# The order of the small matmuls of two half-height heads in the attention stages: pairs side by side, or one head after the other

## The chip, the cores and the metric

The kernel runs on one core of a Trainium2 chip. The metric is device time of one launch, in microseconds (us), the median of the runs. A lower time is better.

## The reference

A decoder of three layers on one sequence of 256 tokens with 1024 features, all in fp32. Layer one: a conformer convolution, cross attention to a memory of 256 tokens, a gated MLP. Layer two: differential attention, cross attention, a gated MLP. Layer three: a sparse attention of 16 heads, then a gated MLP with a short convolution. Two of the attentions matter here, and both have heads of 64 features:

```python
# differential attention: 8 heads, each with two score maps, causal
s = einsum('bqhcd,bkhcd->bhcqk', q, k) * 64 ** -0.5          # c = 0, 1
p = softmax(where(k_pos <= q_pos, s, -inf))
a = p[:, :, 0] - lam * p[:, :, 1]
o = einsum('bhqk,bkhe->bqhe', a, v)                          # e = 128 wide

# third layer: 8 heads with three branches (compressed keys, selected blocks,
# window 512), gated and added, and 8 heads with a window of 128 and a sink
o_nsa = g0 * o_cmp + g1 * o_slc + g2 * o_win
o_swa = banded_attention(qw, kw, v_sw, 128, sinks)
```

With 256 tokens the selected blocks are all blocks and the window of 512 holds all tokens, so that "selected" and "window" are both plain causal attention, each with keys and values of its own. The compressed branch has 15 keys.

## The kernel before

Activations lie transposed in SBUF, features on the 128 partitions and tokens along the row. 180 tiles of weights (1024 x 256, 1 MB) stream in through two buffers. ScalarE (ACT) rounds each to `whi`, VectorE (DVE) forms the rest `wlo` (lines 979 and 982), and TensorE (PE) takes three fp32r products of each (lines 407 to 409). `PLAN` fixes the order of stages. Each engine has a program written out by hand, and semaphores join them.

Four stages of the plan are attentions: `attn_mem0`, `attn_diff`, `attn_mem1`, `attn_nsa`. Each is a list of units. A unit is one query tile of 128 tokens with two score maps, m = 0 and m = 1:

- `attn_diff`: 8 heads x 2 query tiles = 16 units. m is the map of the pair. Score map m lies in partitions 64m to 64m+63 of q and k. Query tile 0 has 128 keys, query tile 1 has 256.
- `attn_nsa`: 32 units. First 4 pairs of windowed heads ("swa"), 2 query tiles each; then 4 pairs of gated heads, each as slc, win, cmp of query tile 0, then slc, win, cmp of query tile 1. m is the head of the pair: q and k in partitions 64m to 64m+63, and the result in PSUM partitions 64m to 64m+63. cmp has 15 keys.
- `attn_mem0` and `attn_mem1`: 4 units each, with full 128-row operands and no mask.

A unit carries three lists for TensorE:

- "S", line 590: the scores, q.k of map m into its own PSUM bank `sc[:, 2*(n%2)+m]`. An fp32 matmul stands in the profile as two MATMUL records. Only 64 rows of the array are used ("64*128"). Line 595: the masks, added as bf16 matmuls of `ident_b` with a mask matrix on all 128 rows, one for each map (two for swa query tile 1: causal and band).
- "T", line 604: transposes of the probabilities `E` into `tp`, one for each map and tile of keys.
- "PV", line 613: values times probabilities into `acc`. In `attn_nsa` these have 64 columns ("128*64"), map m's in PSUM partitions 64m to 64m+63. A unit with 256 keys has two tiles of keys for each map, and so eight records; one with 128 keys or with cmp has four.

The attention is pipelined over units. In step s TensorE issues S of unit s (after the exp of unit s-2), T of unit s-2 (after the probabilities of s-2 are scaled, and after `PT` of unit s-3 is copied), PV of unit s-3, and at some steps the sums of squares of a finished head (`group_stats`, line 563). DVE takes in step s the maximum of S (line 1218), forms the bias `nb` (line 1226, or 1221 to 1224 for swa), and scales E of unit s-1 (lines 1236 to 1255). ACT takes the two exps of unit s (line 813), then copies `tp` of unit s-2 to `PT` (line 832). After the attention come row sums spread by PE (line 572) and the next projection.

Elsewhere `compressed` (lines 690 and 694) makes the compressed keys and values with a few tiny fp32 matmuls. Line 690 writes two PSUM halves, 0 to 63 and then 64 to 127, with two matmuls of 15 columns for each, all of the first half before those of the second. Line 694 writes only one place at a time.

Of the kernel before, what the change touches and what calls it, by code (L numbers as in the profile page):

```python
# [18 lines left out]
S = 256  # L19
# [128 lines left out]
def build(nc, weights, consts, x_in, mem_in, positions, out):  # L148
    ctx = ExitStack()
    with ctx:  # L150
# [50 lines left out]
        products = SQ[:, 0:8, :], A[:, 18:22, :]  # L201
# [6 lines left out]
        sc = ctx.enter_context(nc.psum_tensor("sc", [P, 4, 2 * S], F32))  # L208
# [90 lines left out]
        def nsa_units():  # L299
            units = []  # L300

            for n, c in enumerate((4, 5, 6, 7, 0, 1, 2, 3)):
                swa = c >= 4
                for qt in range(NT):
                    branches = ["swa"] if swa else ["slc", "win", "cmp"]
                    for b, kind in enumerate(branches):
                        nk = NCMP if kind == "cmp" else (qt + 1) * P
                        u = dict(kind=kind, scale=NSA_SCALE, keys=nk, group=n, slot=Q_SLOT + c, S=[], T=[], PV=[], qt=qt, c=c,
                                 last=qt == NT - 1 and b == len(branches) - 1)
                        kts = 1 if kind == "cmp" else qt + 1  # L310
                        first, end = b == 0, b == len(branches) - 1
                        for m in range(2):
                            r = slice(64 * m, 64 * m + 64)
                            k = {"slc": A[r, KS_SLOT, 0:nk], "win": A[r, KW_SLOT, 0:nk], "swa": A[r, KSW_SLOT, 0:nk],
                                 "cmp": KCm[r, 0:NCMP]}[kind]
                            masks = [(causal_b, nk - P, P)] if kind != "cmp" else [(cmask_b[:, 16 * qt:16 * qt + NCMP], 0, NCMP)]
                            if kind == "swa" and qt == 1:
                                masks.append((band_b, 0, P))
                            u["S"].append(([(A[r, Q_SLOT + c, qt * P:(qt + 1) * P], k)], masks))
                        for kt in range(kts):  # L320
                            for m in range(2):
                                r = slice(64 * m, 64 * m + 64)
                                rows = NCMP if kind == "cmp" else P
                                u["T"].append((m, kt * P, rows, m * S + kt * P))
                                v = (VCm[0:NCMP, 64 * m:64 * m + 64] if kind == "cmp" else
                                     V2[:, kt, {"slc": 0, "win": P, "swa": 2 * P}[kind] + 64 * m:][:, 0:64])
                                u["PV"].append(((r, qt * P, P), v, (rows, m * S + kt * P, P),
                                                first and kt == 0, end and kt == kts - 1))
                        units.append(u)
            return units  # L330

        ATTN = {"attn_mem0": mem_units(0), "attn_diff": diff_units(), "attn_mem1": mem_units(1),
                "attn_nsa": nsa_units()}
        U0, n_units = {}, 0
        for name, _, _ in PLAN:
# [66 lines left out]
        def _(pe):  # L402
# [150 lines left out]
            def group_stats(name, g):  # L553


                norm_name, columns_of = {"attn_diff": ("sub", lambda slot: slot), "attn_nsa": ("out2", lambda slot: slot // 4)}[name]
                slot = [u["slot"] for u in ATTN[name] if u["group"] == g][0] - (Q_SLOT if name == "attn_nsa" else 0)
                pe.wait_ge(s_sq, sq.at(name, g + 1))
                if g == 0:
                    pe.wait_ge(st_used, N0[norm_name])  # L560
                for tt in range(NT):
                    col = 2 * columns_of(slot) + tt
                    mm = pe.matmul(st[:, col:col + 1], SQ[:, slot, tt * P:(tt + 1) * P], ones[:, 0:1],
                                   start=g == tt == 0, stop=g == 7 and tt == NT - 1)
                if g == 7:
                    mm.then_inc(stat_ready, 1)
# [8 lines left out]
            def attention(name, steps={}):  # L575

                units, u0 = ATTN[name], U0[name]
                summed = 8 if "mem" in name else 0
                ends = {u["group"]: k for k, u in enumerate(units)}
                for s in range(len(units) + 3):  # L580
                    if s in steps:
                        steps[s]()
                    if s < len(units):
                        u, n = units[s], u0 + s
                        if n >= 2:
                            pe.wait_ge(exp_done, n - 1)
                        for m, (products, masks) in enumerate(u["S"]):
                            dst = sc[:, 2 * (n % 2) + m, :]
                            for k, (q, key) in enumerate(products):
                                mm = pe.matmul(dst[:, 0:u["keys"]], q, key, start=k == 0,  # L590
                                               stop=k == len(products) - 1 and not masks)
                        for m, (products, masks) in enumerate(u["S"]):
                            dst = sc[:, 2 * (n % 2) + m, :]
                            for k, (mask, c0, w) in enumerate(masks):
                                mm = pe.matmul(dst[:, c0:c0 + w], ident_b[:, :], mask if w < P else mask[:, :],
                                               start=False, stop=k == len(masks) - 1)
                        mm.then_inc(s_done, 1)
                    if 2 <= s < len(units) + 2:
                        u, n = units[s - 2], u0 + s - 2
                        pe.wait_ge(p_ready, n + 1)  # L600
                        if n >= 1:
                            pe.wait_ge(pt_ready, n)
                        for m, c0, w, to in u["T"]:
                            mm = pe.transpose(tp[0:w, to:to + P], E[:, n % 3, m, c0:c0 + w], ident)  # L604
                        mm.then_inc(t_done, 1)
                    if s >= 3:
                        u, n = units[s - 3], u0 + s - 3
                        g = G0[name] + u["group"]
                        pe.wait_ge(pt_ready, n + 1)
                        pe.wait_ge(acc_free, g + 1)  # L610
                        for (rows, c0, w), v, (kn, p0, pw), first, last in u["PV"]:
                            dst = acc[g % 2][:, :, :].rearrange("p a b -> p (a b)")
                            mm = pe.matmul(dst[rows, c0:c0 + w], v, PT[0:kn, n % 2, p0:p0 + pw], start=first, stop=last)  # L613
                        mm.then_inc(pv_done, 1)

                    if summed < 8 and s >= ends[summed] + 7 and (name == "attn_diff" or s > 10):
                        group_stats(name, summed)
                        summed += 1
                while summed < 8:
                    group_stats(name, summed)  # L620
                    summed += 1
# [76 lines left out]
            pe.wait_ge(rot_used, ROT0["win"] + ROTS["win"])  # L698

            attention("attn_nsa", {3: turn_hidden, 7: compressed, 10: lambda: pe.wait_ge(cmp_ready, 1)})  # L700
            spread("out2", [(2 * b + tt, sc[:, 0, b * S + tt * P:][:, 0:P]) for b in range(2) for tt in range(NT)])
            stage("wout", Ohi, Olo, source="outn")
# [981 lines left out]
```

## Time and profile before

| | us |
|---|---|
| median of 3 runs | 1386.43 (1385.04 to 1391.51) |
| the profiled execution: its own time | 1386.43 |
| the profiled execution: span of the instructions | 1384.7 |
| outside the span | 1.7 |
| PE busy in the span | 1268.0 (92%) |
| DVE busy | 918.8 (66%) |
| ACT busy | 586.5 (42%) |
| `attn_diff`, first score matmul to last transposed product | 574.7 to 616 |
| `attn_nsa`, first score matmul to last sum of squares | 1015.1 to 1112 |

Times in the views are us from the start of the span. A row of the timeline merges like instructions ("x4") and gives the start of the first and the time until the end of the last; ends of matmuls are modelled, starts are measured. "PEclk" is the share of TensorE's full clock that was granted: 1.00 is 2.4 GHz and 0.50 is 1.2 GHz.

### The profile page before, as it was taken

The numbers are of one execution on the slowest core, as the hardware profiler recorded it, in microseconds if no ns is written. First come the engines' busy times: TensorE is split into PE (matmuls) and PEld (weight loads), VectorE is DVE, ScalarE is ACT, GpSimd is POOL, SyncE is SP. The second block draws the span as 40 slices with busy tenths as digits, with TensorE's granted clock in tenths as the row PEclk, the third lists the DMA queues.
The fourth block names the chain that finished last, engine by engine and source line by source line (L and its number), as shares of the span: only waits on it lengthen the run. The fifth ranks groups of instructions, "written<-read, shape, count | busy, mean of one in ns | idle before, by whom it ended". The sixth has DMA issues, their size and how long they took to land.

```text
span 1384.7 us, 25070 instructions
## 1 busy us (share of the span) xinstructions
PE 1268.0 (92%) x9306; PEld 1184.1 (86%) x9306; DVE 918.8 (66%) x1654; ACT 586.5 (42%) x1003; POOL 61.9 (4%) x52
## 2 busy tenths in 40 slices
PE   5899998899999999878999999999978976999996
PEld 5888888799999999758889999998855575999995
DVE  5885437566666577665656666567875556999955
ACT  3644345444444532443344444442354433344441
POOL 0455200000000000000000000000000000000000
PEclk9999999999999999878999999999976577999998
DMA  6334354244555544402414555562440012344561
GB/s 251 122 122 151 122 182 153 91 153 152 182 182 192 204 152 157 148 1 84 160 65 171 183 182 181 192 211 95 148 153 1 1 60 75 139 172 161 182 212 63
DMA packets 29589, 194.19 MB, mean 140 GB/s; under 512 B 3152, under 2 KB 6352, under 8 KB 6352
## 3 DMA queue, kind: packets, MB, share of 16 engines
q1 hardware_dynamic: 29520, 193.22, 39.9%
q8 instruction: 49, 0.80, 0.2%
q14 instruction: 20, 0.16, 0.0%
HBM read 192.16 MB, written 1.05 MB: 140 GB/s over the span
## 4 chain that ended last, share of the span: by engine, by line
PE 68%; DVE 20%; issue 6%; ACT 3%; DVEq 1%; DMA 0%; ACTq 0%; SPq 0%
PE acc L407 17%; PE acc L409 17%; PE acc L408 17%; PE acc L423 8%; DVE wlo L982 4%; PE acc L613 3%; PE sc L590 2%; DVE wlo L979 2%; PE tp L604 2%; ACT whi L719 1%; DVE E L1177 1%; DVE nw L1030 1%; DVE nw L1031 1%; DVE mx L1218 1%; ACT E L813 1%
## 5 line engine op out<-in xcount | busy, mean ns | idle before, releaser
L407 PE MATMUL acc<-Hhi,whi 128*128 128x256 f32 x1504 | 437.3, 291 | 39.1 <-DVE wlo L982 24.2
L408 PE MATMUL acc<-Hlo,whi 128*128 128x256 f32 x1504 | 428.8, 285 | 0.0
L409 PE MATMUL acc<-Hhi,wlo 128*128 128x256 f32 x1504 | 428.7, 285 | 0.0
L719 ACT ACTIVATE whi<-raw 128x1024 fp32r<-128x1024 f32 x164 | 173.4, 1057 | 479.6 <-PE acc L409 452.7
L407 PEld LDWEIGHTS acc<-Hhi,whi 128*128 128x128 f32 x1504 | 292.1, 194 | 47.1 <-issue 23.7
L408 PEld LDWEIGHTS acc<-Hlo,whi 128*128 128x128 f32 x1504 | 292.3, 194 | 2.4 <-issue 2.2
L979 DVE TENSOR_TENSOR wlo<-raw,whi 128x1024 fp32r<-128x1024 f32 x164 | 201.3, 1228 | 137.7 <-ACT whi L719 136.3
L409 PEld LDWEIGHTS acc<-Hhi,wlo 128*128 128x128 f32 x1504 | 291.9, 194 | 0.0
L407 PE MATMUL acc<-FH,whi 128*128 128x256 f32 x848 | 243.2, 287 | 20.5 <-DVE wlo L982 4.7
L409 PE MATMUL acc<-FH,wlo 128*128 128x256 f32 x848 | 242.6, 286 | 0.0
L982 DVE TENSOR_TENSOR wlo<-raw,whi 128x1024 fp32r<-128x1024 f32 x164 | 200.9, 1225 | 0.0
L407 PEld LDWEIGHTS acc<-FH,whi 128*128 128x128 f32 x848 | 165.3, 195 | 23.1 <-issue 14.6
L720 ACT ACTIVATE whi<-raw 128x1024 fp32r<-128x1024 f32 x164 | 171.1, 1043 | 0.0
L409 PEld LDWEIGHTS acc<-FH,wlo 128*128 128x128 f32 x848 | 164.7, 194 | 0.0
L408 PE MATMUL acc<-FL,whi 128*128 128x256 f32 x528 | 149.0, 282 | 0.0
L408 PEld LDWEIGHTS acc<-FL,whi 128*128 128x128 f32 x528 | 99.6, 189 | 0.0
L408 PE MATMUL acc<-FH,whi 128*128 128x256 f32 x320 | 93.9, 293 | 0.0
L813 ACT ACTIVATE E<-sc,nb 128x256 f32<-128x256 f32 (+2 forms) x112 | 44.5, 402 | 64.9 <-DVE nb L1226 53.9
L408 PEld LDWEIGHTS acc<-FH,whi 128*128 128x128 f32 x320 | 65.0, 203 | 0.0
L423 PE MATMUL acc<-raw,MEM 128*128 128x256 f32 x256 | 55.7, 379 | 0.0
L423 PE MATMUL acc<-MEM,raw 128*128 128x256 f32 x256 | 55.5, 379 | 0.2 <-DVE TG L1114 0.2
L1308 DVE SCALAR_TENSOR_TENSOR sc<-A,cst,sc 128x256 f32<-128x256 f32 x136 | 54.7, 482 | 0.7 <-DVE A L1328 0.5
(213 smaller groups left out, 1588.8 us busy)
## 6 DMA issues: line engine op xcount, KB each, us to landing
raw<-weights SPq DMA_DIRECT2D x180, 1024.0 KB, 4.9
cst<-consts SPq DMA_DIRECT2D x1, 1126.0 KB, 12.0
X<-x_in SPq DMA_DIRECT2D x1, 1024.0 KB, 5.8
MEM<-mem_in SPq DMA_DIRECT2D x1, 1024.0 KB, 14.2
out<-X SPq DMA_DIRECT2D x4, 256.0 KB, 2.2
PT<-positions SPq DMA_DIRECT2D x1, 128.0 KB, 14.0
cst<-consts SPq DMA_DIRECT2D x1, 32.0 KB, 1.9
```

The lines of the kernel that those rows point to most:

```text
L407: pe.matmul(dst, w, x, start=first, stop=False)
L408: pe.matmul(dst, w, xl, start=False, stop=False)
L409: return pe.matmul(dst, wl, x, start=False, stop=last)
L423: mm = pe.matmul(acc[j][:, m, :], x[:, o] if turned else w[:, o], w if turned else x, start=c == 0, stop=c == KC - 1)
L590: mm = pe.matmul(dst[:, 0:u["keys"]], q, key, start=k == 0, stop=k == len(products) - 1 and not masks)
L613: mm = pe.matmul(dst[rows, c0:c0 + w], v, PT[0:kn, n % 2, p0:p0 + pw], start=first, stop=last)
L719: act.activation(whi[j][:, 0:HALF, :], raw[j][:, 0:HALF, :], ACT.Copy).then_inc(hi_out, 1)
L720: act.activation(whi[j][:, HALF:KC, :], raw[j][:, HALF:KC, :], ACT.Copy).then_inc(hi_out, 1)
L813: ins = act.activation(E[:, n % 3, m, 0:u["keys"]], sc[:, 2 * (n % 2) + m, 0:u["keys"]], ACT.Exp, bias=nb[:, n % 2, m:m + 1], scale=u["sca ...
L979: dve.tensor_tensor(out=wlo[j][:, 0:HALF, :], in0=raw[j][:, 0:HALF, :], in1=f(whi[j][:, 0:HALF, :]), op=ALU.subtract)
L982: dve.tensor_tensor(out=wlo[j][:, HALF:KC, :], in0=raw[j][:, HALF:KC, :], in1=f(whi[j][:, HALF:KC, :]), op=ALU.subtract).then_inc(lo_dve, 1)
L1308: ins = dve.scalar_tensor_tensor(out=dst[k], in0=taps(tap), scalar=w, in1=dst[k], op0=ALU.mult, op1=ALU.add)
```

## The change

Two lists are put in another order; no operation is added, removed or resized.

1. In every attention, S and masks were issued as: scores of m = 0, scores of m = 1, masks of m = 0, masks of m = 1. After: scores and masks of m = 0, then scores and masks of m = 1.
2. In `attn_nsa`, T and PV were issued with the tile of keys outside and m inside (k0 m0, k0 m1, k1 m0, k1 m1). After: m outside (k0 m0, k1 m0, k0 m1, k1 m1). A unit with one tile of keys has the same order in both.

```diff
-                        kts = 1 if kind == "cmp" else qt + 1
-                        first, end = b == 0, b == len(branches) - 1
                         for m in range(2):
                             r = slice(64 * m, 64 * m + 64)
 ...
                             u["S"].append(([(A[r, Q_SLOT + c, qt * P:(qt + 1) * P], k)], masks))
-                        for kt in range(kts):
-                            for m in range(2):
-                                r = slice(64 * m, 64 * m + 64)
+                            first, end = b == 0, b == len(branches) - 1
+                            kts = 1 if kind == "cmp" else qt + 1
+                            for kt in range(kts):
                                 rows = NCMP if kind == "cmp" else P
                                 u["T"].append((m, kt * P, rows, m * S + kt * P))
 ...
                             for k, (q, key) in enumerate(products):
                                 mm = pe.matmul(dst[:, 0:u["keys"]], q, key, start=k == 0,
                                                stop=k == len(products) - 1 and not masks)
-                        for m, (products, masks) in enumerate(u["S"]):
-                            dst = sc[:, 2 * (n % 2) + m, :]
                             for k, (mask, c0, w) in enumerate(masks):
                                 mm = pe.matmul(dst[:, c0:c0 + w], ident_b[:, :], mask if w < P else mask[:, :],
                                                start=False, stop=k == len(masks) - 1)
```

## Rows read from the trace of the kernel before

**Rows 1.** The page: busy time and share of each engine.
```profile
PE 1268.0 (92%) x9306; PEld 1184.1 (86%) x9306; DVE 918.8 (66%) x1654; ACT 586.5 (42%) x1003; POOL 61.9 (4%) x52
```

**Rows 2.** Chain that ended last, memk and attn_diff: start, us, what.
```profile
75.47 76.24 PE acc L423 x352
...
590.17 0.63 PE sc L590 x4
...
594.58 0.63 PE sc L590 x4
```

**Rows 3.** Busy us by stretch of the attentions: PE, PEld, DVE, ACT, POOL, PEclk, DMA.
```profile
577.50:587.50 10.00, 8.55 (x38) 5.41 (x38) 7.69 (x27) 5.06 (x23) 0.00 (x0) 0.50 0.31 107
588.00:608.00 20.00, 14.03 (x113) 10.54 (x113) 17.43 (x62) 12.43 (x55) 0.00 (x0) 1.00 0.00 0
...
1035.00:1051.50 16.50, 12.51 (x126) 8.22 (x124) 12.17 (x55) 10.10 (x42) 0.00 (x0) 1.00 0.00 1
1052.50:1115.00 62.50, 57.07 (x315) 36.03 (x315) 30.49 (x141) 24.60 (x103) 0.00 (x0) 0.50 0.00 1
```

**Rows 4.** Timeline of PE, parts of attn_nsa, full clock.
```profile
1015.13 0.49 PE L590 MATMUL sc<-A 64*128 64x128 f32 x4
1015.55 0.28 PE L595 MATMUL sc<-causal_b,ident_b 128*128 128x128 bf16 x2
1015.77 0.70 PE L590 MATMUL sc<-A 64*128 64x256 f32 x4
1016.40 0.23 PE L595 MATMUL sc<-causal_b,ident_b 128*128 128x128 bf16 x1
1016.47 0.22 PE L595 MATMUL sc<-band_b,ident_b 128*128 128x128 bf16 x1
...
1043.54 0.49 PE L590 MATMUL sc<-A 64*128 64x128 f32 x4
```

**Rows 5.** Timeline of PE, parts of attn_nsa, clock 0.50.
```profile
1026.54 0.29 PE L595 MATMUL sc<-causal_b,ident_b 128*128 128x128 bf16 x1
1026.62 0.31 PE L595 MATMUL sc<-band_b,ident_b 128*128 128x128 bf16 x1
...
1055.25 0.80 PE L590 MATMUL sc<-A 64*128 64x128 f32 x4
...
1066.07 1.22 PE L590 MATMUL sc<-A 64*128 64x256 f32 x4
1067.22 0.40 PE L595 MATMUL sc<-causal_b,ident_b 128*128 128x128 bf16 x2
...
1068.63 0.61 PE L590 MATMUL sc<-KCm,A 64*128 64x15 f32 x4
...
1071.64 0.80 PE L590 MATMUL sc<-A 64*128 64x128 f32 x4
1072.37 0.40 PE L595 MATMUL sc<-causal_b,ident_b 128*128 128x128 bf16 x2
```

**Rows 6.** Timeline of PE, transposes that waited after their step's scores.
```profile
584.16 0.45 PE L604 MATMUL tp<-cst,E 128*128 128x128 f32 x1 [0.28 <-ACT PT L832]
...
593.43 0.30 PE L604 MATMUL tp<-cst,E 128*128 128x128 f32 x1 [1.06 <-ACT PT L832]
...
1030.25 0.66 PE L604 MATMUL tp<-cst,E 128*128 128x128 f32 x2 [0.57 <-ACT PT L832]
...
1050.64 0.38 PE L604 MATMUL tp<-cst,E 128*15 128x128 f32 x2 [0.42 <-ACT PT L832]
...
1070.00 1.09 PE L604 MATMUL tp<-cst,E 128*128 128x128 f32 x4 [0.60 <-ACT PT L832]
```

**Rows 7.** Timeline of PE, products into PSUM halves.
```profile
1037.59 0.41 PE L690 MATMUL st<-HCm,cst 128*64 128x15 f32 x8
1037.93 0.62 PE L694 MATMUL st<-cst,HCm 128*15 128x64 f32 x8
...
1073.55 1.12 PE L613 MATMUL acc<-PT,A 128*64 128x128 f32 x8
```

## The prediction

> **What bounds the kernel now.** The page's first part comes first: PE is busy for 92% of the span, so TensorE is the engine to look at, but a share over the whole span says nothing of the two stages that change [rows 1]. The chain of work that ended last says what sets the time there. In attn_diff it goes round once for each head: the scores of the 256-key unit (0.63 us), its masks, DVE's maximum, ACT's exps and copy to PT, and then PE again, 4.4 us later [rows 2]. So the scores of query tile 1 are on the path in every head, and those of query tile 0 lie beside DVE and ACT. The stretches then show the clock: attn_diff ran at 0.50 in its first 10 us and at 1.00 in the next 20; attn_nsa at 1.00 from 1035 to 1051.5 and at 0.50 from there to its end, with PE busy for 57.07 of 62.50 us [rows 3]. In that last stretch PE itself is the path, but for one wait of 0.60 us in each head. The timeline of PE gives the prices at both clocks [rows 4, 5] and the waits that can cover something [rows 6].
>
> What the reader is to see in the timeline: from the first score matmul of a unit to its first mask, four "64*128" records take 0.63 us at full clock with 256 columns (1015.77 to 1016.40) and 0.42 with 128 (1015.13 to 1015.55) [rows 4]. The four are two maps with two passes each. What do 128 columns cost in one pass? In the plain fp32 stream of memk 352 records of 256 columns take 76.24 us, 0.217 each, so 0.108 for 128 columns [rows 2]. Four passes in turn would cost 0.43 us more with 256 columns than with 128; two would cost 0.22. The difference of the two blocks is 0.21. So the two maps of a unit, one in the upper and one in the lower half of the array's rows, run side by side, and the pair costs what one map alone would.
>
> **The change part by part.**
>
> *Scores and masks.* The mask of map 0 works on all 128 rows and now stands between the two score matmuls. It can't run beside a half-height matmul: at each change of form there is a gap. So map 1's scores no longer run beside map 0's, but after them. A unit had scores (pair), mask, mask; it gets scores, mask, scores, mask. Added: one more block of scores with its step to the mask, plus the step from mask to scores, less the step from mask to mask.
> - Full clock: from mask (second of the pair, 0.07 after 1015.55) to the next scores at 1015.77 is 0.15 us; mask to mask is 0.07 (1016.40 to 1016.47) [rows 4]. A 256-key unit gets 0.63 + 0.15 - 0.07 = 0.71 us longer, a 128-key unit 0.42 + 0.08 = 0.50, cmp at most that.
> - Half clock: blocks of 1.15 (1066.07 to 1067.22), 0.73 (1071.64 to 1072.37) and for cmp 0.54 (its records span 0.61, and the modelled spans of the others run 0.07 over their blocks) [rows 5]. Mask to mask is 0.08 [rows 5]. The step from mask to scores isn't shown at this clock; it lies between the full clock's 0.15 and twice that. The fixed part of a block (1.15 less twice 0.42 for what 128 columns add, against 0.63 less twice 0.21) is 0.31 against 0.21, a factor of 1.5, so I take 0.23. That gives 1.30, 0.88 and 0.70.
>
> No other engine gets more work. DVE and ACT wait for the last mask of the unit as before, only later. Behind the scores on PE's queue stand T of unit s-2 and PV of unit s-3; where T waited for PT anyway, the added time of that same step is covered up to the wait [rows 6].
>
> attn_diff, 16 units. The first two lie under DVE's work on the next weights: nothing. At half clock units 3 to 6: 0.88, 1.30, 0.88 less a wait of 0.28, 1.30; 4.1 us. At full clock the four 256-key units on the path cost 0.71 each, 2.8 us; the 128-key units (0.50) fit under waits such as 1.06 [rows 6]. The last 256-key unit falls where the clock changes: 1.0. Together 7.9 us.
>
> attn_nsa, windowed heads, 8 units: first two again nothing. Then 0.88, 1.30, 0.88 - 0.57 [rows 6], 1.30, nothing (its wait is long enough), 0.71: 4.5 us.
>
> attn_nsa, gated heads, 24 units. The first head is mostly at full clock: slc nothing, win 0.50, cmp nothing, then 0.71, 0.71 less a wait of 0.42 [rows 6], 0.70 for cmp: 2.2 us. Each of the other three at half clock: twice 0.88, 0.70, twice 1.30, and 0.70 less the wait of 0.60 [rows 6]: 5.2 us, together 15.5.
>
> Sum for the scores: 7.9 + 4.5 + 2.2 + 15.5 = 30.1 us. If the steps between forms cost nothing, each unit would be 0.08 to 0.15 cheaper, 3 us over the 24 units that count; if the mask-to-scores step cost double, 4 us more.
>
> *Transposes.* Same records, all full-height, one after the other in either order, released by the same probabilities and read by one copy: nothing. PE's queue itself is their cover; there is none to lose.
>
> *PV of attn_nsa.* Only the 12 units with 256 keys change. Here the two maps go to the two halves of PSUM's partitions: eight records take 1.12 us at half clock (1073.55), where one after the other would take 8 x 0.21 = 1.7. They too run two by two. After, all four records of map 0 come before the four of map 1. Would they still overlap? Line 690 is this very order: four records into the first half, then four into the second. Its eight span 0.41 us; line 694's eight, all into one place, span 0.62 [rows 7]. With a modelled length of about 0.2 a record, line 694's step is 0.06, and four records alone would span 0.38. So map 1 starts about one step after map 0, long before its last record. I price that step at 0.1 us a unit, 1 us in all, and at nothing from below. The upper bound is no overlap but for the last record, three passes more: 0.64 us each in the nine units at half clock and 0.32 in the three at full, 6.7 us.
> The Trainium skill, "TensorE: Matmul & The Clock Gate", Part 3, The mechanism, says that only weight loads are pulled ahead and matmuls run strictly in order. By that rule the PV term would be the upper bound, and the forecast 6 us higher. By that rule line 690's eight records would have taken as long as line 694's; the row disagrees, at 15 columns, and no row shows this order at 128.
>
> *Clock.* Units get longer, so stretches at full clock of the same length hold fewer of them: about half a head in attn_diff and a third of a gated head in attn_nsa go over to half clock, at 2 and 8 us a head (below). Some of that may be won back where such a stretch comes later. I take 1.5 us, between nothing and the first rival.
>
> **Sum.** 30.1 + 1 + 1.5 = 32.6 us on 1386.4, the profiled execution's own time, which is also the median of the runs: 1419.
>
> **The rivals.**
> - *The clock stays at half in both stages.* Rows 3 show that it moves within them, and the change makes other work of each us. A head of attn_diff goes round in 4.4 us at full clock [rows 2] and, as an estimate, in 5.2 at half: the block of scores grows from 0.63 to 1.15 and the products behind it by some 0.3. After, 5.1 and 5.2 + 1.30 + 0.60 = 7.1. Four and a half heads lose 2.0 us each: 9 us. In attn_nsa a gated head takes 16.4 us at half clock (1055.25 to 1071.64) [rows 5] and the first, mostly at full, 11.7 (1043.54 [rows 4] to 1055.25); after, 21.6 and 13.9, so the first loses 7.7. Less the 1.5 us already counted: 1434. For it: 0.50 was granted for 62.5 us though PE was busy for 57. Against: in attn_diff the clock rose after just such busy 10 us.
> - *Strict order in PV*, as above: 1425.
> - *Half the cost is covered.* If the chain had more slack than PE's waits show, or each second block loaded its weights during the mask (0.1 to 0.2 us a unit), a third to a half of the 32.6 would go: 1405. Against: in the 62.5 us at half clock PE idles for 5 us, of which I have taken the waits.
> - *The change does nothing.* If map 1's scores could start beside map 0's in spite of the mask between them, the pair would stay a pair: 1387. Against: every unit has its 0.15 us from mask to scores, where mask to mask takes 0.07; forms don't mix [rows 4].
> - *Full clock throughout*, and no loss. After, a gated head would take 13.9 us against 16.4 before, three times: -7.5. The 10 us from the last scores of attn_nsa to its end, all at half before, would give 4 more. Against these stand +0.71 for each of seven 256-key units in attn_diff less 0.8 for each of two and a half heads there (+3), +1 for the windowed heads, +2.2 for the first gated head: 1385. It decides only if 1.00 is granted from 1052 on, for at least three heads.
>
> **How the numbers follow.** Forecast as summed 0.55, half clock 0.15, strict PV 0.10, half covered 0.13, nothing 0.04, full clock 0.03. The likeliest case has its own range of 1412 to 1427 (the steps between forms, -3 and +4, the clock term, and PV). To leave out no more than 2 in 10 the range goes from the covered case to the half clock: 1404 to 1434. About 0.5% (7 us) is what a measurement of this kernel can tell from no change. Slower by more: 0.55 + 0.15 + 0.10 + 0.13 = 0.93. Within: the last two, of which the full clock could give a little more than worked out, 0.05. Faster: 0.02.
>
> **What would show it.** In the timeline, each unit of attn_diff and attn_nsa shows line 590 x2, line 595 x1, line 590 x2, line 595 x1, with about 0.63 us from first scores to first mask at full clock and 1.15 at half for 256 columns: the same as for the pair now. If that first block were much shorter than the pair's, the two maps had not been running side by side, and the main term would be wrong. The waits of rows 6 shrink or go. attn_mem0 and attn_mem1 don't change. Line 613's eight records stay near 1.1 us at half clock; 1.8 would be strict order. The stages between and after move by nothing but their start. The prediction fails if the granted clock in attn_nsa differs, for that moves more than any other term.

## The result, and the profile after

The changed kernel takes 1430.21 us (median of 4 runs, 1429.55 to 1431.63), the kernel before 1387.28 in the same runs: a ratio of 1.031, 95% interval 1.029 to 1.033, or 43 us more. The forecast was slower, 1419 us, with a range of 1404 to 1434. The profiled execution has a span of 1428.1 us. In the experiments below one of the four runs of the kernel with scores and masks alone took 1821.7 us at a mean granted clock of 0.637; it belongs to a slow state and is left out of that kernel's ratio.

The page's first part, the busy time of each engine, after. PE has 58 us more of it with the same 9306 matmuls [rows 1]:

```profile
PE 1326.5 (93%) x9306; PEld 1218.2 (85%) x9306; DVE 919.7 (64%) x1654; ACT 586.8 (41%) x1003; POOL 61.7 (4%) x52
```

The stretches of the two attentions, after (length, then PE, PEld, DVE, ACT, POOL, granted clock, DMA share, GB/s). They answer to [rows 3]. All four stretches have 0.50, where before 20 us of attn_diff and 16.5 of attn_nsa had 1.00. Only the first units of each attention, ahead of these stretches, still had full clock:

```profile
577.50:587.50 10.00, 10.00 (x32) 6.02 (x32) 6.11 (x22) 4.27 (x19) 0.00 (x0) 0.50 0.22 90
588.00:608.00 20.00, 20.00 (x70) 13.57 (x69) 11.47 (x39) 7.73 (x33) 0.00 (x0) 0.50 0.00 0
...
1036.00:1052.00 16.00, 14.46 (x56) 8.32 (x56) 8.61 (x37) 5.96 (x28) 0.00 (x0) 0.50 0.25 100
1052.50:1157.00 104.50, 102.14 (x445) 63.52 (x442) 42.83 (x193) 35.98 (x148) 0.00 (x0) 0.50 0.00 1
```

The timeline of PE, after, in new line numbers (588 scores, 591 masks, 600 transposes, 609 products with the values). First units 0 and 1 of attn_nsa, still at full clock, as [rows 4]; then a part of a gated head at half clock, as [rows 5] and [rows 7]:

```profile
1029.42 0.49 PE L588 MATMUL sc<-A 64*128 64x128 f32 x2
1029.84 0.23 PE L591 MATMUL sc<-causal_b,ident_b 128*128 128x128 bf16 x1
1030.00 0.48 PE L588 MATMUL sc<-A 64*128 64x128 f32 x2
1030.42 0.23 PE L591 MATMUL sc<-causal_b,ident_b 128*128 128x128 bf16 x1
1030.58 0.70 PE L588 MATMUL sc<-A 64*128 64x256 f32 x2
1031.21 0.23 PE L591 MATMUL sc<-causal_b,ident_b 128*128 128x128 bf16 x1
...
1032.12 0.22 PE L591 MATMUL sc<-band_b,ident_b 128*128 128x128 bf16 x1
...
1084.77 0.79 PE L588 MATMUL sc<-A 64*128 64x128 f32 x2
1085.49 0.29 PE L591 MATMUL sc<-causal_b,ident_b 128*128 128x128 bf16 x1
1085.71 0.79 PE L588 MATMUL sc<-A 64*128 64x128 f32 x2
1086.44 0.29 PE L591 MATMUL sc<-causal_b,ident_b 128*128 128x128 bf16 x1
1086.52 1.06 PE L600 MATMUL tp<-cst,E 128*128 128x128 f32 x4
...
1095.35 1.22 PE L588 MATMUL sc<-A 64*128 64x256 f32 x2
1096.51 0.29 PE L591 MATMUL sc<-causal_b,ident_b 128*128 128x128 bf16 x1
1096.72 1.22 PE L588 MATMUL sc<-A 64*128 64x256 f32 x2
...
1105.97 0.79 PE L588 MATMUL sc<-A 64*128 64x128 f32 x2
...
1108.71 1.13 PE L609 MATMUL acc<-PT,A 128*64 128x128 f32 x8
```

Two records now take as long as four did. One map's scores to its mask are 0.42 us with 128 columns and 0.63 with 256 at full clock (1029.42 to 1029.84, 1030.58 to 1031.21), and 0.72 and 1.16 at half: the blocks of the pair before [rows 4, 5]. From mask to the next scores it is 0.16 us at full clock and 0.22 at half (1085.49 to 1085.71). A gated head takes 21.2 us (1084.77 to 1105.97) where it took 16.4 [rows 5]. The eight records of PV span 1.13 us, before 1.12 [rows 7]. Two more rows of the timeline before are needed below, the last mask of unit 1 at full clock and the transposes behind the masks of 1072.37 at half:

```profile
1016.58 0.22 PE L595 MATMUL sc<-band_b,ident_b 128*128 128x128 bf16 x1
...
1072.56 1.06 PE L604 MATMUL tp<-cst,E 128*128 128x128 f32 x4
```

By stage, from the first score matmul to the first spread of row sums (line 572, now 570): attn_diff 574.69 to 620.39 before, 573.18 to 635.43 after, so 45.7 and 62.3 us, +16.6. attn_nsa 1015.13 to 1114.26 before, 1029.42 to 1158.23 after, so 99.1 and 128.8, +29.7. All else together is 2.8 us shorter. These are single executions, and a stage that is left as it was differs from one to the next, in length and in clock. The traces of all kernels here that have one kind of scores throughout a stage, longest last (us, and mean granted clock of the whole stage):

| scores in the stage | attn_diff | attn_nsa |
|---|---|---|
| half-height, old order | 45.7 at 0.75, 46.8 at 0.73, 47.4 at 0.70, 49.9 at 0.62 | 99.1 at 0.62, 99.6 at 0.62, 101.5 at 0.61, 102.3 at 0.58 |
| half-height, new order | 62.3 at 0.52 in three kernels | 128.2 at 0.52, 128.5 at 0.52, 128.8 at 0.53 |
| full-height (experiments 3 and 5) | 43.4 at 0.96, 44.8 at 0.91, 45.8 at 0.86, 45.8 at 0.87 | 90.3 at 0.84, 93.8 at 0.81, 94.2 at 0.80, 95.0 at 0.80, 98.6 at 0.76 |

The new order stands for the changed kernel and those of experiment 1 with its scores in the stage. The trace of the kernel before is the shortest of its row in both stages. So the change costs 12 to 17 us in attn_diff and 26 to 30 in attn_nsa, and the differences of 16.6 and 29.7 lie at the upper end.

### The profile page after: what moved, and what is told of

Same layout as the page of the kernel before. It is cut to its first block, busy times and chain, and to the rows that moved or that the text cites. A ratio compares the mean times of both kernels' runs of the same rounds, so it can differ in the third digit from the quotient of the medians.

```text
span 1428.1 us, 25070 instructions
## 1 busy us (share of the span) xinstructions
PE 1326.5 (93%) x9306; PEld 1218.2 (85%) x9306; DVE 919.7 (64%) x1654; ACT 586.8 (41%) x1003; POOL 61.7 (4%) x52
## 4 chain that ended last, share of the span: by engine, by line
PE 72%; DVE 18%; issue 5%; ACT 2%; DVEq 1%; DMA 1%; ACTq 0%; SPq 0%
PE acc L405 17%; PE acc L407 16%; PE acc L406 16%; PE acc L421 8%; PE sc L588 6%; DVE wlo L978 4%; PE acc L609 3%; PE tp L600 2%; DVE wlo L975 2%; PE sc L591 1%; ACT whi L715 1%; DVE E L1173 1%; DVE nw L1027 1%; DVE nw L1026 1%; PE st L561 1%
## 5 line engine op out<-in xcount | busy, mean ns | idle before, releaser
L406 PEld LDWEIGHTS acc<-FL,whi 128*128 128x128 f32 x528 | 99.6, 189 | 0.0
L588 PE MATMUL sc<-A 64*128 64x128 f32 (+1 forms) x160 | 77.6, 585 | 6.7 <-ACT ske L813 5.2
L1214 DVE TENSOR_REDUCE mx<-sc 128x2 f32<-128x512 f32 (+2 forms) x56 | 29.3, 524 | 82.2 <-PE sc L591 78.1
```

Source lines behind the costliest of these rows:

```text
L406: pe.matmul(dst, w, xl, start=False, stop=False)
L588: mm = pe.matmul(dst[:, 0:u["keys"]], q, key, start=k == 0, stop=k == len(products) - 1 and not masks)
L1214: link(dve.reduce_max(mx[:, r, :], sc[:, 2 * r:2 * r + 2, 0:u["keys"]], axis=AX_X))
```

## The experiments

Medians and ratios are against runs of the kernel before on the same chip. In the fences of windows the first row covers 33 us of attn_diff, the second 60 us of attn_nsa. In the kernel before the granted clock of these two windows is 0.84 and 0.60, after the change 0.50 and 0.50.

**1. Which part of the change costs.** Four kernels, with the old order but for one part. Scores and masks alone; without the second loop head the masks fall inside the loop over m:

```diff
                                                stop=k == len(products) - 1 and not masks)
-                        for m, (products, masks) in enumerate(u["S"]):
-                            dst = sc[:, 2 * (n % 2) + m, :]
                             for k, (mask, c0, w) in enumerate(masks):
```

> Only the order of scores and masks is changed (map by map); T and PV keep the order of the kernel before. If the whole cost is the pair of half-height score matmuls that no longer runs side by side, with the clock that is lost on the way, this is as slow as the changed kernel: 1430 us, with the clock at 0.50 from 575 to 640 and from 1036 to 1169. If the order of PV has a part in it (strict order of matmuls), it is 4 to 7 us faster than that, 1424 us.

Measured: 1430.8 us, ratio 1.031 (1.028 to 1.034). This part is the whole cost.

Transposes and PV alone (the first half of the change's diff, with the scores as before):

> Only T and PV of attn_nsa are in the new order; scores and masks keep the old one. If the two PSUM halves still run side by side when one map's four records come before the other's: 1387 us, eight records in 1.1 us at half clock. If matmuls start strictly in order: eight records in 1.8 us, 1393 us.

Measured: 1388.6 us, ratio 1.001 (1.000 to 1.003). Timeline of PE of this kernel, half clock; the eight records span 1.13 us, not 1.8:

```profile
1077.66 1.06 PE L602 MATMUL tp<-cst,E 128*128 128x128 f32 x4
1078.66 1.13 PE L611 MATMUL acc<-PT,A 128*64 128x128 f32 x8
```

So the two PSUM halves overlap although one half's four records come first. Strict order is out, at 128 columns too. The prediction had set against the row a rule of the Trainium skill, "TensorE: Matmul & The Clock Gate", Part 3, The mechanism, that matmuls run strictly in order. The trace disagrees with it for this order of column halves, by 1.13 us against 1.8.

Scores and masks by map in one stage each (`if name == "attn_nsa"`, or `"attn_diff"`, around the new order):

> Scores and masks map by map in attn_nsa alone. From the traces of before and after, attn_nsa grew by 29.7 us from first scores to the spread of row sums, and attn_diff by 16.6. If each stage loses for itself: 1416 us, attn_diff as before, clock at 0.50 through attn_nsa. If the long stretch at half clock in attn_diff makes that in attn_nsa worse (or the other way round): attn_nsa grows by less, 1409 us.

> Scores and masks map by map in attn_diff alone. If each stage loses for itself: 1402 to 1404 us, attn_diff at half clock throughout, attn_nsa as before. Direct price alone (7.9 us, the clock as before the change) would be 1395 us.

Measured: 1415.5 us, ratio 1.020 (1.018 to 1.022), +27 us; and 1400.4 us, ratio 1.009 (1.007 to 1.011), +12 us. Together 40 of 43 us: each stage loses for itself, attn_diff 2 us less than expected. That expectation had taken the 16.6 us of two single traces, and 12 us is in line with the 12 to 17 of the table above. Windows of the kernel with attn_diff alone: its own stage is at 0.50, attn_nsa at 0.64, about as before.

```profile
575.00:608.00 33.00, 32.44 (x107) 20.78 (x105) 19.92 (x66) 13.62 (x57) 0.00 (x0) 0.50 0.09 33
1040.00:1100.00 60.00, 54.71 (x354) 34.68 (x354) 35.16 (x156) 28.20 (x121) 0.00 (x0) 0.64 0.01 2
```

**2. A grouping whose direct price is covered.** Only the 128-key units of attn_diff in the new order:

```diff
+                        by_map = name == "attn_diff" and u["keys"] == P
```

> Scores and masks map by map only in the eight 128-key units of attn_diff. At full clock their 0.50 us lie under a wait of about 1.1 us, so that the direct cost is 1.5 us (the units at half clock). If serial half-height scores are what keeps the clock at 0.50, attn_diff runs at half throughout and a head takes 5.2 us and something instead of 4.4: 1393 to 1396 us. If the clock only moved for reasons of its own: 1389 us.

Measured: 1391.6 us, ratio 1.003 (1.001 to 1.005). The windows:

```profile
575.00:608.00 33.00, 30.73 (x132) 21.59 (x133) 22.54 (x79) 15.36 (x67) 0.00 (x0) 0.55 0.09 33
1040.00:1100.00 60.00, 55.63 (x344) 35.93 (x344) 32.20 (x145) 27.45 (x117) 0.00 (x0) 0.60 0.00 1
```

The clock of attn_diff went from 0.84 to 0.55 with half of its units changed, and the time to between the two expectations. Part of that fall is chance: in the same window of three other kernels that leave attn_diff as it was, the clock is 0.67, 0.74 and 0.79. But 0.55 lies below them all. Here attn_diff takes 53.0 us (572.43 to 625.39), 3 to 7 more than the 45.7 to 49.9 of the old order, where the direct price was put at 1.5. So the new order seems to lower the granted clock in this stage, beside its direct price; the three kernels with all units in the new order, at 0.52 for the whole stage, say the same more plainly.

**3. Scores without half-height matmuls.** The score matmuls take all 128 rows, in the old order and in the new one. Both maps get the sum of the two score matrices, which differs from the reference; numbers and widths of matmuls stay.

```diff
-                        u["S"].append(([(A[r, h, qt * P:(qt + 1) * P], A[r, 8 + h, 0:nk])],
+                        u["S"].append(([(A[:, h, qt * P:(qt + 1) * P], A[:, 8 + h, 0:nk])],
```

> Every score matmul of attn_diff and attn_nsa takes all 128 rows of q and k in place of its own 64, so that both maps get the sum of the two score matrices: what it computes differs, the number and width of matmuls doesn't. Order as before the change. The two maps can't run side by side, but there is no change of form between scores and masks either. If the lost overlap is most of the cost and the change of form the smaller part: at full clock a 256-key block takes 0.9 us instead of 0.63, a gain of 0.1 us or so comes back at the step to the masks; at half clock 1.7 instead of 1.15 less 0.13. About 0.1 to 0.4 us a unit, 1394 us at the clock of before. If changes of form are most of the cost, it is no slower than before, 1384 us or less. The clock may go either way here; at 1.00 throughout attn_nsa it would be under 1375 us in both theories.

> Scores on all 128 rows for each map (both maps get the sum of the two score matrices, as in the kernel with full-height scores in the old order), but scores and masks map by map, as in the changed kernel. If the order costs only because it separates two half-height matmuls and changes the form twice more, it costs nothing here: 1379 us, within 0.5% of the same kernel in the old order. If the order itself holds something up (masks that wait on their scores, PSUM banks taken in turn), it is some 30 us slower than that, 1410 us.

Measured: 1378.8 us, ratio 0.993 (0.991 to 0.996), in the old order; 1381.9 us, ratio 0.997 (0.995 to 0.999), in the new. Timeline of PE of both at full clock, first old, then new:

```profile
593.09 1.11 PE L590 MATMUL sc<-A 128*128 128x256 f32 x4
594.04 0.28 PE L595 MATMUL sc<-causal_b,ident_b 128*128 128x128 bf16 x2
594.15 0.39 PE L604 MATMUL tp<-cst,E 128*128 128x128 f32 x2
```

```profile
593.57 0.68 PE L590 MATMUL sc<-A 128*128 128x256 f32 x2
594.09 0.22 PE L593 MATMUL sc<-causal_b,ident_b 128*128 128x128 bf16 x1
594.14 0.65 PE L590 MATMUL sc<-A 128*128 128x256 f32 x2
594.63 0.22 PE L593 MATMUL sc<-causal_b,ident_b 128*128 128x128 bf16 x1
594.68 0.39 PE L602 MATMUL tp<-cst,E 128*128 128x128 f32 x2
```

Here the order costs 0.05 us a unit (1.11 us from scores to transposes, against 1.06) and perhaps 3 us in all: nearly nothing. It costs only where it parts two half-height matmuls. From a bf16 mask to the next fp32 scores it is 0.05 us here (594.09 to 594.14), where it was 0.16 to half-height scores: so the step comes with the change of height and not with the change of type. The other reading was new to me. From first scores to first mask a 256-key block of four full-height records takes 0.95 us where the half-height pair takes 0.63; and yet the kernel is faster. The windows of the kernel in the old order say why (its trace is of the slowest of its 8 runs):

```profile
575.00:608.00 33.00, 22.25 (x165) 19.13 (x165) 27.99 (x93) 19.88 (x80) 0.00 (x0) 1.00 0.11 41
1040.00:1100.00 60.00, 54.80 (x359) 39.83 (x357) 34.58 (x156) 28.38 (x121) 0.00 (x0) 0.76 0.00 1
```

The clock is 1.00 and 0.76, where it was 0.84 and 0.60. Over 8 runs of this kernel time and mean clock go together: 1371.6 us at 0.967, 1384.4 at 0.957. All traces of kernels with full-height scores in a stage have a higher clock there than all those with half-height scores (the table above). Neither of the two readings that I had written down fits: the lost overlap is the larger part of the direct price, as the first said, and the time is nevertheless that of the second, through the clock, which the expectation had left open.

**4. Is it the mask between them?** The changed kernel with `masks = []` for every unit of attn_diff and attn_nsa, so that attention sees all keys:

> The changed kernel with all masks of attn_diff and attn_nsa left out, so that attention sees all keys. Now nothing full-height stands between the scores of map 0 and map 1. If that was what parted the pair: they run side by side again, a 256-key block takes 0.63 us at full clock for both maps, and the time is that of the kernel before less 104 masks of 0.07 to 0.1 us, 1376 to 1387 us. If grouping by map parts them anyway: above 1415 us.

Measured: 1387.2 us, ratio 0.998 (0.997 to 1.000). Timeline of PE, half clock:

```profile
575.78 0.80 PE L589 MATMUL sc<-A 64*128 64x128 f32 x4 [3.02 <-ACT E L810]
...
577.35 1.23 PE L589 MATMUL sc<-A 64*128 64x256 f32 x4
...
592.65 1.22 PE L589 MATMUL sc<-A 64*128 64x256 f32 x4
593.81 0.69 PE L601 MATMUL tp<-cst,E 128*128 128x128 f32 x2
```

Four records take 0.80 and 1.23 us, as before the change [rows 5], and 1.16 us from scores to the next form: the pair is side by side again, with the same loops over maps as in the changed kernel. The full-height matmul between them is what parts them. The 104 masks that are left out bring nothing measurable in the median. This trace is of the fastest of 10 runs, 1378.7 us: attn_nsa took 91.2 us in it, 8 fewer than in the kernel before, but attn_diff 50.2 us at a mean clock of 0.53, 4.5 more than in the trace before. So not only serial scores can go with half clock.

**5. A version that gives the right result.** Keys of map m are copied to a tile with zeros in the other map's 64 rows, so that scores can take all 128 rows. GpSimd copies them while PE works on the projections before; `step` issues one such operation and waits for its end. Once for attn_nsa alone, once for both stages, in the old order:

```diff
+            pool.wait_ge(rot_used, ROT0["diffq"])
+            for m in range(2):
+                r, o = slice(64 * m, 64 * m + 64), slice(64 - 64 * m, 128 - 64 * m)
+                step(pool.memset(KZD[o, 8 * m:8 * m + 8, :], 0.0))
+                step(pool.tensor_copy(KZD[r, 8 * m:8 * m + 8, :], A[r, 8:16, :]))
...
-                        u["S"].append(([(A[r, h, qt * P:(qt + 1) * P], A[r, 8 + h, 0:nk])],
+                        u["S"].append(([(A[:, h, qt * P:(qt + 1) * P], KZD[:, 8 * m + h, 0:nk])],
```

> Old order. In attn_nsa the keys of each map lie in a tile of their own with zeros in the other half (copied by GpSimd, which is idle, before the attention), and scores take all 128 rows: the same result as the reference, no change of form between scores and masks, no matmuls side by side. Following the full-height kernel, whose granted clock was 0.957 to 0.967 against 0.935 to 0.944 of the kernel before: 1383 us if attn_nsa brings half of its 8 us. If its gain came from attn_diff alone, or if the copies delay the first unit: 1387 to 1389 us.

> The same in attn_diff too (16 tiles of padded keys, copied by GpSimd during the projections before). If the gain of full-height scores doesn't hang on its wrong keys: 1379 us, faster than the kernel before by 0.4 to 0.8%. If copying 2048 columns twice on GpSimd ends after the first unit is due, or takes the SBUF port from DVE: 1390 us or more.

Measured: 1381.1 us, ratio 0.995 (0.993 to 0.997), and 1380.5 us, ratio 0.995 (0.993 to 0.997). The gain doesn't hang on wrong keys. All that can be measured of it comes with attn_nsa: in attn_diff the clock rises too, but the stage takes 45.8 us, as long as before, since its score matmuls are longer. The copies are early: GpSimd's groups of the second kernel show 7.6 us of them for attn_diff, and they start at 534.0, 40 us before the first score matmul.

```profile
L416 POOL COPY KZD<-A 64x2048 f32<-64x2048 f32 x2 | 4.0, 1976 | 0.1
L415 POOL MEMSET KZD<- 64x2048 f32 x2 | 3.6, 1804 | 383.6 <-DVE A L1154 383.5
```

Then one matmul for both maps, with the queries as shared weights and the two padded keys as up to 512 columns of one PSUM bank, and one matmul for both masks (`both_maps(n)` is `sc[:, 2 * (n % 2), :]` as two maps of 256 columns):

```diff
+                            dst = both_maps(n)
+                            pe.matmul(dst[:, :, 0:u["keys"]], q, u["keyz"], start=True, stop=False)
+                            for k, (mask, c0, w) in enumerate(masks):
+                                mm = pe.matmul(dst[:, :, c0:c0 + w], ident_b[:, :], mask[:, 0:w].unsqueeze(1).broadcast_to((P, 2, w)),
+                                               start=False, stop=k == len(masks) - 1)
```

> Padded keys in both stages, and one score matmul of up to 512 columns for both maps (the queries are the shared weights), both maps in one PSUM bank, and one matmul for both masks: the same result. Two records in place of four for the scores. Against the kernel with padded keys: cmp units fall from four weight loads of about 0.2 us to two (8 units, 2 to 3 us at half clock), the others keep their columns and lose only loads that were hidden. 1377 us if that counts and the clock stays as it was there; 1381 us if cmp's scores lie under the wait for PT; above 1385 us if DVE's and ACT's reading of one bank for both maps, or the clock, takes it back.

Measured: 1376.6 us, ratio 0.993 (0.990 to 0.995): the fastest kernel here that computes the reference, 0.7% below the kernel before and 54 us below the changed one. The windows, and a 256-key unit of attn_diff at full clock:

```profile
575.00:608.00 33.00, 22.49 (x112) 14.05 (x113) 27.89 (x93) 19.69 (x76) 0.00 (x0) 0.95 0.14 52
1040.00:1100.00 60.00, 50.70 (x309) 30.58 (x307) 34.45 (x158) 29.63 (x124) 0.00 (x0) 0.83 0.00 1
```

```profile
599.09 1.10 PE L624 MATMUL sc<-KZD,A 128*128 128x512 f32 x2
600.03 0.27 PE L626 MATMUL sc<-causal_b,ident_b 128*128 128x256 bf16 x1
```

Its step over the kernel with padded keys (4 us) is within the intervals of both.

## Why the prediction was right, and what it mis-sized

- *The two maps of a unit run side by side, and the mask between them parts them*: right. The blocks after are those of the pair [rows 4, 5], and without masks the pair is back (experiment 4). The prices were 0.63 + 0.15 - 0.07 at full clock and 0.15 to 0.30, taken as 0.23, for the step from mask to scores at half; measured 0.16 and 0.22. The first two units of attn_nsa had full clock before and after: from first scores to last mask the one with 128 keys grew by 0.51 us and the one with 256 by 0.73 (1016.58 less 1015.77 before, 1032.12 less 1030.58 after), priced 0.50 and 0.71 (its two masks a map move with the scores).
- *Where it costs*: right in kind, a little high in size. A gated head at half clock was to lose 5.2 us and lost 4.8. Two masks in a row took 0.19 us to the next transposes (1072.37 to 1072.56), 0.11 of it from the second; the one at the end of a unit now takes 0.08 (1086.44 to 1086.52), and the sum left that out. The cmp units also lost less than their 0.70. The bound of -3 us for the steps between forms counts 24 units, where the sum prices 33; with the steps of all of them it would be -4.
- *PV, 1 us*: nothing beyond noise (1.001, 1.000 to 1.003), and the eight records span what they did. The bound of strict order (6.7 us in place of 1) is out.
- *Transposes and other stages*: nothing, as said; outside the two stages the profiled execution was 2.8 us shorter.
- *The clock, 1.5 us*: this is the term that was mis-sized. The likeliest case had both stages keep their stretches at full clock; they lost them all. With the three heads of attn_nsa at their measured 4.8 us each and PV at nothing, the direct price is 7.9 us in attn_diff and 21.0 in attn_nsa. Of the 43 us measured that leaves 14 for the clock, an estimate from these prices. By the single traces it is 5 to 9 us in each stage (12 to 17 less 7.9, 26 to 30 less 21.0). The rival "the clock stays at half in both stages" had reckoned 9 and 7.7 by the same rows. That rival, given 0.15, is what happened: it gave 1434, and without the 1 us for PV and the 1.2 us too much for three heads 1432, against 1430 measured. So the time fell in the stated range only because the range had been drawn out to this rival: the likeliest case's own range of 1412 to 1427 doesn't hold it. The rival should have had a larger part: the row of 62.5 us at 0.50 with PE busy was there to read [rows 3], and I let the rise after the first 10 us of attn_diff weigh more.
- *The rivals "half covered", "nothing" and "full clock throughout"*: none happened. In attn_diff even the units under waits ended up on the path: at half clock PE was busy for all of 588 to 608, and a head took 7.2 us. The sum of "full clock throughout" was also wrong: its own terms (-7.5, -4, +3, +1, +2.2 on 1386.4) give 1381, not 1385. Nothing hung on it.

What isn't shown is why the clock is granted or not. The traces show that it goes with the height and order of the scores within these stages, and that a kernel whose score blocks are each longer can win by it; experiment 4 shows half clock in attn_diff without any serial scores. The split of the 43 us into direct price and clock rests on the prices at either clock in the rows, not on a run of the changed order at full clock: there was none, beyond its first two units.

## What to carry to other kernels

Two half-height matmuls in different halves of the array run side by side, but not with a full-height one between them, as the masks here: group by form first, by head second. Whoever moves matmuls about in a stage where the granted clock wavers should price the stage at both levels and give the lower one a real chance. And a pair side by side isn't the end of it: zeros in the keys made the scores 0.3 us a unit longer at the same clock, and the kernel faster.

## What the runs showed of the hardware that wasn't expected

- Full-height scores, with more PE time a unit, came with a higher granted clock in every trace that has them: 0.86 to 0.96 over attn_diff and 0.76 to 0.84 over attn_nsa, against 0.62 to 0.75 and 0.58 to 0.62 with half-height scores in the old order. With nothing else changed the kernel was 0.7% faster (1378.8 us).
- Four matmuls into one half of PSUM's partitions followed by four into the other take as long as two and two in turn: 1.13 against 1.12 us for eight records of 128 columns at half clock.
- After a full-height mask of 128 columns a half-height matmul starts 0.16 us later at full clock and 0.22 at half, instead of 0.07 and 0.08 for another such mask; with full-height scores the order of scores and masks costs 0.05 us a unit.
